# GpSimd adds the next attention step's bias ahead of this step's shift difference and low part

## What is computed

```python
xn = _rms_norm(h, mix_norm[l]); proj = xn @ w_in[l]
# attention: per block i of 128 queries (4 of them), 8 heads of 64
head_scores = relu(einsum('bqhd,bsd->bqhs', qib, k_idx32) * IDX_DIM ** -0.5)
scores = einsum('bqhs,bqh->bqs', head_scores, wib) * IDX_HEADS ** -0.5   # causal, then the 128 best keys
_, sel = lax.top_k(scores, topk)
logits = einsum('bqhd,bqkhd->bhqk', qb, k_sel) * scale
bias = rel_bias32[_t5_bucket(q_pos - sel)]                                # one value per head and distance
logits = where(valid, logits + bias, -inf)
probs = softmax(logits);  out = einsum('bhqk,bqkhd->bqhd', probs, v_sel)
# RWKV branch, beside it
z_prev = pad(z, ((0,0),(1,0),(0,0)))[:, :-1];  z = z + mu * (z_prev - z)
# gates of the merge
merged = sigmoid(gate_attn) * (y_attn @ w_branch_attn) + sigmoid(gate_rwkv) * (y_rwkv @ w_branch_rwkv)
```

## Time and profile before

| what | value |
|---|---|
| median of 3 runs | 3371.89 us (3371.63, 3371.89, 3383.97) |
| the profiled execution's own time | 3382.12 us |
| its span | 3380.2 us, mean granted TensorE clock 0.94 |
| busy in the span | PE 3016.8 us (89%), DVE 1417.1 us (42%), ACT 1173.6 us (35%), POOL 1203.2 us (36%) |
| the 32 attention steps | about 267 to 459 us from the span's start |

### The profile page before, as it was taken

One profiled execution on the slowest core, in us unless ns is written; L12 is line 12 of the kernel. 1 busy time (PEld: TensorE's weight loads), 2 busy tenths in 40 slices (PEclk: granted clock), 3 DMA queues, 4 the chain that ended last, 5 costly groups with the idle time before them and its releaser, 6 DMA issues.

```text
span 3380.2 us, 40151 instructions
## 1 busy us (share of the span) xinstructions
PE 3016.8 (89%) x15600; PEld 2341.2 (69%) x15600; DVE 1417.1 (42%) x2055; ACT 1173.6 (35%) x1681; POOL 1203.2 (36%) x559
## 2 busy tenths in 40 slices
PE   7989776879999998889999999889669777999998
PEld 5856535758888885667888887647457556788886
DVE  3017536445321373332273446050577342656442
ACT  4243242244222336333342224323433532542222
POOL 3413322114444442424544443304104122544442
PEclk9988777989999999899999999979889799999999
DMA  3312110023232332215422222202102111522222
GB/s 125 96 66 72 47 38 1 3 105 101 94 99 94 107 123 73 97 51 168 150 94 96 97 94 100 87 25 91 38 29 82 52 46 43 207 102 94 94 99 81
DMA packets 80666, 284.06 MB, mean 84 GB/s; under 512 B 8968, under 2 KB 9096, under 8 KB 79744
## 3 DMA queue, kind: packets, MB, share of 16 engines
q1 hardware_dynamic: 66240, 236.36, 21.0%
q10 hardware_dynamic: 13296, 41.97, 3.3%
q0 software_dynamic: 976, 3.56, 0.3%
HBM read 260.86 MB, written 20.99 MB: 83 GB/s over the span
## 4 chain that ended last, share of the span: by engine, by line
PE 55%; issue 19%; DVE 11%; POOL 9%; ACT 5%; DMA 1%; POOLq 0%; SPq 0%; ACTq 0%; DVEq 0%
PE bank L331 15%; PE bank L333 14%; PE bank L332 14%; POOL slab_r L2681 8%; PE bank L551 2%; PE bank L529 1%; PE bank L438 1%; PE bank L605 1%; DVE work L2475 1%; DVE work L2134 1%; DVE small L2132 1%; PE bank L819 1%; DVE work L2121 0%; PE bank L878 0%; DVE work L2357 0%
## 5 line engine op out<-in xcount | busy, mean ns | idle before, releaser
L2681 POOL TENSOR_TENSOR slab_r<-slab,slab_high 128x1024 fp32r<-128x1024 f32 x442 | 1094.3, 2478 | 1762.8 <-ACT slab_high L1093 1762.6
L331 PE MATMUL bank<-xh,slab_high 128*128 128x512 f32 x2256 | 908.2, 403 | 35.5 <-POOL slab_r L2681 31.1
L333 PE MATMUL bank<-xh,slab_r 128*128 128x512 f32 x2256 | 889.6, 394 | 0.0
L332 PE MATMUL bank<-x_raw_r,slab_high 128*128 128x512 f32 x2064 | 816.1, 395 | 0.0
L1093 ACT CAST slab_high<-slab 128x1024 fp32r<-128x1024 f32 x442 | 462.8, 1048 | 448.1 <-DMA slab<-in_w_down 215.5
L332 PE MATMUL bank<-work_r,slab_high 128*128 128x512 f32 x1376 | 546.2, 397 | 0.0
L331 PEld LDWEIGHTS bank<-xh,slab_high 128*128 128x128 f32 x2256 | 431.4, 191 | 148.8 <-POOL slab_r L2681 34.8
L331 PE MATMUL bank<-work_r,slab_high 128*128 128x512 f32 x1184 | 473.5, 400 | 50.3 <-DVE work_r L1874 24.9
L333 PEld LDWEIGHTS bank<-xh,slab_r 128*128 128x128 f32 x2256 | 430.9, 191 | 93.6
L333 PE MATMUL bank<-work_r,slab_r 128*128 128x512 f32 x1184 | 474.1, 400 | 0.0
L332 PEld LDWEIGHTS bank<-x_raw_r,slab_high 128*128 128x128 f32 x2064 | 395.5, 192 | 80.7 <-issue 1.7
(11 more groups left out here) (465 smaller groups left out, 2889.3 us busy)
## 6 DMA issues: line engine op xcount, KB each, us to landing
slab<-in_w_down SPq DMA_DIRECT2D x88, 512.0 KB, 3.2
slab<-in_w_up SPq DMA_DIRECT2D x64, 512.0 KB, 3.2
slab<-in_w_gates SPq DMA_DIRECT2D x56, 512.0 KB, 3.3
slab<-in_w_merge SPq DMA_DIRECT2D x48, 512.0 KB, 3.7
slab<-in_w_gu SPq DMA_DIRECT2D x44, 512.0 KB, 3.5
slab<-in_w_in_a SPq DMA_DIRECT2D x32, 512.0 KB, 3.5
gates<-staging ACTq DMA_DIRECT2D x56, 256.0 KB, 2.2
slab<-in_w_out SPq DMA_DIRECT2D x24, 512.0 KB, 3.2
```

The lines of the kernel that those rows point to most:

```text
L331: first = pe.matmul(bank[b][:, :], wh, mh, start=start, stop=False)
L332: pe.matmul(bank[b][:, :], wh, ml, start=False, stop=False)
L333: end = pe.matmul(bank[b][:, :], wl, mh, start=False, stop=stop)
L2681: pool.tensor_tensor(slab_low[:, slot, :], slab[:, slot, :], plain(slab_high[:, slot, :]), ALU.subtract).then_inc(S("slab_split"), 1)
```

## The change

The bias add becomes a function `biases(g)`. It is called once for step 0 before the loop; then iteration g first calls `biases(g + 1)` and only after it does its own shift difference and low part. The waits of the bias add are unchanged, except that the wait for `relu_used` is tied to g = 0 and that for `mask_ready` to h = 0 of the later blocks, and that all of them now stand one iteration earlier in POOL's list, ahead of that iteration's shift difference and low part. The instructions and their number are the same; no DMA is moved.

```diff
-            g = 0
-            for i in range(NT):
+            steps = [(i, h) for i in range(NT) for h in range(8)]
+
+            def biases(g):
+
+                i, h = steps[g]
                 w = (i + 1) * P
-                if i == 0:
+                if g == 0:
                     pool.wait_ge(S("relu_used"), n.next(S("relu_used"), 8 * (NT - 1)))
-                else:
+                elif h == 0:
                     pool.wait_ge(S("mask_ready"), n.next(S("mask_ready")))
-                for h in range(8):
-                    if g >= 2:
-                        pool.wait_ge(evac_by["dve"], handed_at["attention"]["dve"] + g - 1)
-                    m = C("caus") if i == 0 else work[:, mask_at[i]:mask_at[i] + w]
-                    pool.tensor_tensor(W(55 + g % 2)[:, 0:w], W(40 + h)[:, 3 * P - i * P:3 * P - i * P + w], m,
-                        ALU.add)\
-                        .then_inc(S("bias_ready"), n.up(S("bias_ready")))
-
-                    k = g - (SHIFT_FROM - 1)
-                    if 0 <= k < len(shift_tiles):
...
-                    gate_lows(IN_ATTENTION)
-                    g += 1
+                if g >= 2:
+                    pool.wait_ge(evac_by["dve"], handed_at["attention"]["dve"] + g - 1)
+                m = C("caus") if i == 0 else work[:, mask_at[i]:mask_at[i] + w]
+                pool.tensor_tensor(W(55 + g % 2)[:, 0:w], W(40 + h)[:, 3 * P - i * P:3 * P - i * P + w], m, ALU.add)\
+                    .then_inc(S("bias_ready"), n.up(S("bias_ready")))
+
+            biases(0)
+            for g in range(len(steps)):
+                if g + 1 < len(steps):
+                    biases(g + 1)
+
+                k = g - (SHIFT_FROM - 1)
+                if 0 <= k < len(shift_tiles):
+                    if k >= 2:
+                        pool.wait_ge(S("shift_done"), n.next(S("shift_done")))
+                    z, o = W(shift_tiles[k]), W(38 + k % 2)
+                    pool.tensor_scalar(o[:, 0:1], z[:, 0:1], -1.0, None, ALU.mult).then_inc(chain, n.up(chain))
+                    pool.tensor_tensor(o[:, 1:T], z[:, 0:T - 1], z[:, 1:T], ALU.subtract)\
+                        .then_inc(S("shift_diff"), n.up(S("shift_diff")))
+                gate_lows(IN_ATTENTION)
```

## The result

| | before | after |
|---|---|---|
| median, 13 runs each | 3380.92 us (3371.63 to 3383.97) | 3355.68 us (3350.15 to 3371.65) |
| ratio | | 0.9934, 95% interval 0.9924 to 0.9944 |
| the profiled execution's own time | 3382.12 us | 3353.23 us |
| first to last add (line 2107) of the 32 attention steps | 181.32 us | 151.70 us |

The kernel is 0.66% faster, 25.2 us by the medians and 28.9 by the two profiled executions. The add still stands on line 2107; the bias add moved to line 2742, the shift difference to 2755 and 2756.

A forecast was written before the change was run, and what follows sets the result against it. Bound: a closed loop in the 32 attention steps, POOL waiting for DVE's shift and DVE's add for POOL's bias. 21.0 + 7.4 + 2.2 - 2.5 = 28.1 us off 3371.9 gives 3344 us, own range 3338 to 3349, wide range 3336 to 3358.

The forecast's parts named there:

- Part 1: Steps 17 to 22: DVE's six waits for POOL's bias add vanish and DVE sets the pace, 21.0 us gained.
- part 5: Port shared by DVE and POOL: POOL's work beside DVE's scaling costs nothing to 0.2 us per step; taken as nothing.
- Part 2: Steps 23 to 30: with the bias out of the way PE sets the pace at 5.45 us, 7.4 us gained.
- Part 3: Steps 13 to 16: low part moves behind the mask, mask instruction shortens and PE's gates stay fast, 2.2 us gained.
- Part 4: PE's clock in the 384-key steps: falls after idle times near 1.8 us, one exposed low step, 2.5 us lost.
- rival B: Clock costs more: three low 384-key steps and one fall after step 22, 19 us gained, 3353 us; chance 0.15.
- Rival A: POOL wins the port, DVE's scaling waits in steps 17 to 22: 18 us gained, 3354 us; chance 0.12.
- rivals C and D: C: DVE waits for PE's logits instead, 3363 us, chance 0.08; D: PE stays at 1.2 GHz, 3403 us, chance 0.03.

The follow-up runs named there:

- a_again: The changed kernel traced and timed once more, nothing altered: ratio 0.9928 to the kernel before, median 3357.35 us, adds 0 to 31 in 154.3 us.
- i: Changed kernel plus three unused DVE maxima in each of steps 17 to 22: adds 0 to 31 in 165.4 us, median 3375.18 us.
- d: Changed kernel with only the biases of steps 24 to 31 moved ahead, the others left behind the low part: ratio 0.9967 to before, median 3373.38 us.
- c: Changed kernel with only the biases up to step 23 moved ahead, the others left behind the low part: ratio 0.9925 to before, median 3358.58 us.
- j: Changed kernel plus three unused DVE maxima in each of steps 24 to 30: adds 0 to 31 in 155.5 us, median 3372.07 us.
- e: Changed kernel with only the biases of steps 17 to 31 moved ahead, old order up to step 16: adds 0 to 31 in 153.9 us, median 3354.03 us.
- f: Changed kernel with POOL's low part put right after the next bias, ahead of the shift difference: ratio 0.9917 to before, median 3349.58 us.
- b: Changed kernel with the next bias put between POOL's shift difference and low part: ratio 1.0 to before, median 3386.94 us.
- h: f with PE's early gate products per step set to 4, then 5 in steps 17 to 22, then 4 or 3: median 3348.97 us.
- l: h run once more with more runs: ratio 0.9912 to before, median 3352.15 us, adds 0 to 31 in 151.7 us.
- k: b plus two unused DVE maxima in each of steps 17 to 22: adds 0 to 31 in 178.3 us, median 3379.42 us.

## Why the prediction was right or wrong

**Direction and mechanism: right.** The wait for the bias is gone, the parts are there one by one; the time was not, for a reason that comes last. From the two traces, add to add:

| part | forecast | measured |
|---|---|---|
| 1, adds 17 to 23 | 21.0 | 58.46 - 37.62 = 20.8 |
| 2, adds 23 to 31 | 7.4 | 48.96 - 42.16 = 6.8 |
| 3, first add to add 17 | 2.2 | 73.90 - 71.92 = 2.0 |
| 4, clock | -2.5 | 0 in this execution, -2.6 in a_again |
| sum | 28.1 | 29.6, and 27.0 in a_again |

*Part 1*: i shows that DVE is the bound there, d that the waits come back with the order. That 20.8 comes so near to 21.0 is partly luck: between adds 17 and 23 five scalings took 0.19 us longer each (part 5), 0.95 us that the forecast left out, but without a wait the rows of DVE overlap by some 0.08 us (the shift at 345.06 ends at 345.81, the next add starts at 345.73) where 0.05 us was to stay between them, 0.8 us gained in six steps. *Part 2*: c and j. *Part 3*: e.

*Part 4* had about the right size, in some executions only, and not in the right place. The 2.5 us were for a low step on 384 keys. In the first profile PE did fall to the low level there, in step 21, after 1.59 us idle, and DVE's slack hid it whole (the add of step 23 did not wait). In a_again it fell one step later, after 1.96 us idle (granted clock 0.52 from 379.2 to 382.3), and this came out at the next adds: that is rival B's fall after step 22, which was put at about 4 us and cost 2.6. The rule I read out of three idle times does not hold: 1.60 us two steps earlier brought no fall, nor did 1.55 in a_again, while in f PE fell after 1.55 us and not after 2.04. No length of idle time that separates the two comes out of these traces.

*Part 5* I took at nothing. The scaling takes 0.61 us in the narrow steps after the change instead of 0.42, 1.1 us in six steps and within the 0.2 a step that was named, and DVE's shift, which I had not considered at all, is held too. In the changed kernel, with POOL's bias for step 24 beside it:

```profile
379.85 1.75 DVE L2152 SCALAR_TENSOR_TENSOR work<-work,vec 128x512 f32<-128x512 f32 x1
```

```profile
379.67 1.38 POOL L2742 TENSOR_TENSOR work<-work 128x512 f32<-128x512 f32 x1
```

1.75 us instead of 0.75: it ends at 381.60, half a microsecond after POOL's bias. It happened with PE as the bound and cost nothing: the add behind it still waits 0.82 us for PE's logits. In f it was 2.86. The Trainium skill, SBUF — State Buffer, Who interferes with whom, says that a VectorE instruction with two SBUF inputs contends with a GpSimd instruction that reads SBUF, which is this case: the trace agrees. Rival A did not come (DVE went first at every end of a subtraction), but b shows its price, 0.96 us a step, and f 1.7 us in one, when the low part is put where it can start first.

**The step that failed is the last one: from the profiled execution to the median.** I took "the same difference off the median" of 3371.89, which came from three runs of which two were near 3372. Of the 13 runs of before that are known now, ten lie between 3378 and 3384 and the median is 3380.92; the profiled execution, 3382.1, was the usual one and the 10.2 us that I carried over as a constant belonged to a rarer, quicker kind. From 3380.9 the same sum gives 3352.8 us, 2.9 below the measured 3355.7; from 3371.9 it gave 3344, 11.7 below. The forecast's own range of 3338 to 3349 lay 9 us too low with it; the measured time is outside it, nearest to rival A's 3354 and B's 3353, though for neither's reason, and inside 3347 to 3358, the same range on the right level. (Its lower edge doesn't follow from its reasons either: without any fall exposed the sum is 30.6 us and the time 3341, and some tenths don't make 3338 of it.) The traces show of what such differences are made: scores stage 22.8 or 30, entry 31.5, 34 or 37, recurrence 129.6 or 148.8, all by the granted clock. Which of them was quick in the runs at 3372 is not known, as none of those was traced. The scores stage is the likeliest: of 56 later runs of the kernel before six lie between 3371 and 3373 us, all six with a mean clock of 0.945 or 0.946, and the other 50 had 0.941 or less, and in f and h the traced executions with the 22.8 us had 0.950 and 0.949 and were 6 to 8 us quicker than their neighbours at 0.945.

By that the effect itself was forecast at 28.1 and measured at 25.2 by medians, 28.9 by profiles. The 3.7 between these two are in the changed kernel's typical execution, some 2 to 3 us above its profiled one (a low clock as in a_again would do it; that is argued, not shown), and in the one of before, 1.2 below its own. The wide range of 3336 to 3358 and the direction held; rivals C and D did not come about, and of B only the one fall after step 22, in a_again.

## What to carry to other kernels

When an engine's in-order list mixes a small item that another engine waits for with items that this other engine itself releases, put the small one first and ask of each item what releases it. Then look at what it leaves on the other side: in the end only the longest list of each stretch counts, and added work on the one beside it costs a sixth of its length or less (j). And set a forecast against the profiled execution's own level unless the median rests on many runs; a gain of 12 us can be swallowed by an untouched stage that runs at another clock (b), so compare stage by stage before believing a median. Take the whole loop as the stage: l wins 1.6 us by the adds 18 to 31 and nothing by all 32.

## What the runs showed of the hardware

- An untouched stage of small matmuls took 129.6 us at a granted clock of 0.97 or 148.8 at 0.83. Which of them it is goes with what comes before: by their totals, seven of ten runs of b, ten of eleven of j and none of eleven of k were of the long kind (one of each was traced). A coarse shift of the entry time doesn't explain it (i).
- The scores stage, in which PE is busy 28.8 of 30.1 us, took 22.8 us at a granted clock of 1.00 (f, h) or 30.1 at 0.59 (after).
- PE's clock fell after idle times of 1.55 (f), 1.59 (after) and 1.96 us (a_again) and did not after 1.55 (a_again), 1.60 (after) and 2.04 us (f).
- DVE's scaling and mask instruction, and its shift with two inputs from SBUF, are held up by a running POOL instruction to some 0.2 to 0.6 us past its end (scaling 0.21 in b, mask 0.21 in before, shift 0.55 in after and 0.56 in f). The maxima and replacements of the selection rounds kept 0.68 to 0.70 us beside POOL's low part (after, 360.5 to 363.0 us).
